# Five of 22 pairs of upward FFN tiles as seven half-width products, in a two-block transformer kernel on one core

## The reference

```python
D_FF = 2816
def conv_ffn(h, w_up, conv_w, w_down):
    gu = causal_dwconv(h @ w_up, conv_w)
    g, u = jnp.split(gu, 2, axis=-1)
    return (jax.nn.silu(g) * u) @ w_down
...
x = x + conv_ffn(rmsnorm(x, norm_ffn_gain[i]), ffn_w_up[i], ffn_conv_w[i], ffn_w_down[i])
```

## Time and profile before

| | |
|---|---|
| median of 3 runs | 1222.37 us (1222.31 to 1222.84) |
| the profiled execution | 1223.61 us, its span 1221.5 us |
| upward FFN, 22 pairs | about 795 to 1036 us of the span |
| busy share of the span | PE 99%, PEld 81%, DVE 57%, ACT 50%, POOL 57% |

### The profile page before, as it was taken

How to read it: one execution, slowest core, us unless ns; L and a number is a source line. 1 busy time by engine, 2 the same in 40 slices (tenths; PEclk the granted TensorE clock), 3 DMA queues, 4 the chain that set the end, 5 groups by cost and what they waited for, 6 DMA issues and landing times.

```text
span 1221.5 us, 18340 instructions
## 1 busy us (share of the span) xinstructions
PE 1207.6 (99%) x6667; PEld 990.1 (81%) x6667; DVE 698.6 (57%) x1239; ACT 612.0 (50%) x1184; POOL 700.3 (57%) x538
## 2 busy tenths in 40 slices
PE   9999999999999999999999999999999999999997
PEld 7977777777888899987887777878888888889886
DVE  5545426757646777745697555445454545966224
ACT  6355535676644344445634656544444444333544
POOL 8673232353269776855484566545655565886842
PEclk9999999999999999999999999999999999999999
DMA  7432222122223333354142223333333333333332
GB/s 236 107 95 73 70 61 61 52 63 77 70 62 103 95 98 94 107 179 116 52 119 58 58 62 96 96 85 104 87 88 102 103 88 80 101 96 117 108 87 69
DMA packets 62432, 112.22 MB, mean 92 GB/s; under 512 B 6856, under 2 KB 11464, under 8 KB 62344
## 3 DMA queue, kind: packets, MB, share of 16 engines
q1 hardware_dynamic: 62200, 111.06, 32.5%
q10 hardware_dynamic: 144, 0.00, 0.0%
...
## 4 chain that ended last, share of the span: by engine, by line
PE 95%; DVE 3%; ACT 1%; issue 1%; POOL 1%; DMA 0%; SPq 0%; DVEq 0%; POOLq 0%; ACTq 0%
PE pb L1101 23%; PE pb L1102 23%; PE pb L1104 23%; PE pb L1154 3%; PE pb L1156 3%; PE pb L1155 3%; PE pb L1310 2%; PE pb L1286 2%; PE pb L1163 2%; PE pb L1253 1%; PE pb L1224 1%; PE pb L1226 1%; PE pb L1225 1%; PE pb L1207 1%; PE pb L1205 1%; PE pb L1275 1%
## 5 line engine op out<-in xcount | busy, mean ns | idle before, releaser
L2684 POOL TENSOR_TENSOR wlo<-raw,whi 128x512 fp32r<-128x512 f32 (+2 forms) x384 | 518.7, 1369 | 333.2 <-ACT whi L1503 332.2
L1101 PE MATMUL pb<-HH,whi 128*128 128x512 f32 x856 | 345.4, 404 | 0.0
L1102 PE MATMUL pb<-HL,whi 128*128 128x512 f32 x856 | 338.5, 395 | 0.0
L1104 PE MATMUL pb<-HH,wlo 128*128 128x512 f32 x856 | 337.5, 394 | 0.0
L1503 ACT ACTIVATE whi<-raw 128x512 fp32r<-128x512 f32 (+2 forms) x384 | 226.1, 613 | 106.9 <-PE pb L1104 55.7
L1101 PEld LDWEIGHTS pb<-HH,whi 128*128 128x128 f32 x856 | 161.3, 188 | 42.2 <-issue 4.6
L1102 PEld LDWEIGHTS pb<-HL,whi 128*128 128x128 f32 x856 | 161.0, 188 | 38.1 <-issue 2.9
L1104 PEld LDWEIGHTS pb<-HH,wlo 128*128 128x128 f32 x856 | 160.9, 188 | 37.4
L1976 DVE TENSOR_TENSOR pb<-pb,rff 128x512 f32<-128x512 f32 x44 | 30.8, 700 | 124.0 <-PE pb L1104 117.6
L1621 ACT ACTIVATE P<-P,stat 128x256 f32<-128x256 f32 (+3 forms) x96 | 50.5, 527 | 78.7 <-DVE stat L2246 57.1
L2684 POOL TENSOR_TENSOR fl<-cv,fh 128x512 fp32r<-128x512 f32 x22 | 28.9, 1314 | 86.4 <-ACT fh L1897 86.4
...
## 6 DMA issues: line engine op xcount, KB each, us to landing
...
```

The source lines that it names most:

```text
L1101: pe.do.matmul(b, hi, xh[k], start=start, stop=False, skip_group_check=tile[0] == "down")
L1102: pe.do.matmul(b, hi, xl[k], start=False, stop=False, skip_group_check=tile[0] == "down")
L1104: m = pe.do.matmul(b, lo, xh[k], start=False, stop=stop, skip_group_check=tile[0] == "down")
L2684: g.do.tensor_tensor(lo, x, hi.bitcast(F32), ALU.subtract).then_inc(*up(name, point))
```

## The change

`UPS` names the five pairs j = 6, 9, 11, 13 and 15. Their two tiles are made by seven products.

- **Activation sums** `tus`, `tuh`, `tul` for the new pairs are made once, one quarter in each of the pairs j = 1 to 4: ScalarE scales x into SBUF and into two PSUM banks (three copies), VectorE makes four sums of 256 columns, ScalarE one high part of 1024 columns, GpSimd two low parts of 512.
- **A seven-product pair** takes three banks: `ab` (the bank of `("ffn", 0, j)`), `cd`, and `e` (the bank of `("ffn", 1, j)`). ScalarE copies the first product from `ab` to U7 only once S2 is done, and stands with that copy ahead of the split of S4. VectorE then has six instructions on the banks (`product_up`), and `scaled` follows for both tiles behind the last product.
- **Low parts**: in these pairs GpSimd makes that of S3 too, so all seven.
- **Order of steps**: `taps(1, j-1)` and `product(j-1)` move behind the product of S3 in a pair of `UPS`; `product(j-2)` moves from the first half of pair j-1 into its second half, ahead of `scaled(1, j-1)`.

```diff
+UPS = (6, 9, 11, 13, 15)
+NUP = NGATE + len(UPS)
...
         for x in FACTORS:
-            self.split_to(self.unit_of[p, x] + LOOK)
+            if not NGATE <= p < NUP or x not in ("A22", "S2"):
+                self.split_to(self.unit_of[p, x] + LOOK)
             self.add("product7", p, x)
+            if NGATE <= p < NUP and x == "S2":
+                self.split_to(self.unit_of[p, x] + LOOK)
+            if x == "S3" and NGATE <= p < NUP:
+                self.add("taps", 1, UPS[p - NGATE] - 1)
+                self.add("product", UPS[p - NGATE] - 1)
...
+                if half and j + 1 in UPS and j not in UPS:
+                    add("product", j - 1)
                 add("scaled", half, j)
-                if (half, j) != (0, 0):
-                    add("taps", 1 - half, j - 1 + half)
                 if half:
+                    add("taps", 0, j)
                     add("swish", j)
-                elif j:
-                    add("product", j - 1)
+                elif j and j not in UPS:
+                    add("taps", 1, j - 1)
+                    if j + 1 not in UPS:
+                        add("product", j - 1)
...
             def product7(p, x):
-                if p >= NGATE:
+                if kind(p) == "up" and x == "S2":
+                    a.wait_ge(*at("product7", p, x))
+                    a.wait_ge(*at("u3", p - 1))
+                    a.do.activation(U7, ps("ffn", 0, UPS[p - NGATE])[:, 0:H], ACT.Copy).then_inc(*up("a_c7", ("v0", p)))
...
+            def product_up(p, x):
...
+                if x == "S2":
+                    v.wait_ge(*at("v0", p))
+                    v.wait_ge(*at("product7", p, "S2"))
+                    plus(U7, ab[:, right], U7, ("u2", p))
+                elif x == "S3":
+                    v.wait_ge(*at("product7", p, "S3"))
+                    v.wait_ge(*last("v_c7"))
+                    plus(W8, cd[:, left], U7)
+                    plus(ZU, cd[:, right], U7, ("u3", p))
+                    v.wait_ge(*last("v_c7"))
+                    plus(e[:, right], cd[:, right], W8, ("empty", ("cd", j)))
+                    plus(e[:, left], e[:, left], ZU)
+                elif x == "S4":
+                    v.wait_ge(*at("product7", p, "S4"))
+                    plus(ab[:, right], ab[:, right], W8)
...
-                elif factor[1] == "S3":
+                elif factor[1] == "S3" and kind(factor[0]) != "up":
                     return
```

More of the change, by code:

```diff
@@ L618, in second @@
         add("begin3")
+        sums_of = {j + 1: j for j in range(4)}
         for j in range(NPAIR):
+            if j in UPS:
+                for t in (("ffn", 0, j), ("cd", j), ("ffn", 1, j)):
+                    take(t)
+                self.pair(NGATE + UPS.index(j))
             for half in range(2):
-                take(("ffn", half, j))
-                self.proj(("ffn", half, j), "ffn_up", 2816 * half + P * j)
+                if j not in UPS:
+                    take(("ffn", half, j))
+                    self.proj(("ffn", half, j), "ffn_up", 2816 * half + P * j)
                 if j == 0 and half == 0:
@@ L664, in second @@
                 self.hold(DOWN_BANK["tile"][7], ("down", 7))
-            self.pair(NGATE + n)
+            self.pair(NUP + n)
             add("down_out", 2 * n)
@@ L948, in sums_at, with kind @@
             return S7 if p < NGATE else S8
+        def kind(p):
+            return "gate" if p < NGATE else "up" if p < NUP else "down"
         T_AT = {"S1": 0, "S3": 1, "A22": 2, "S2": 3}
@@ L1004, in build @@
         ffn_work = a3.p
+        sums_places = [(ffn_work, ffn_work + 8 * T)] + [(place[f"fh{j}"], place[f"fl{j}"]) for j in (16, 18, 20)]
+        THU, TLU = ([tensor_at(f"tu{n}{kp}", [P, 2 * T], F32R, sums_places[kp][x]) [:, :] for kp in range(4)]
+                    for x, n in enumerate("hl"))
+        TSU = [tensor_at(f"tus{kp}", [P, 2 * T], F32, sums_places[kp][1])[:, :] for kp in range(4)]
+        ZU = tensor_at("zu", [P, H], F32, 226176)[:, :]
         a3.p += 4 * (4 * T + 64)
@@ L2035, in split @@
                     weights("S3", arrived["A11"], arrived["A21"], ALU.subtract)
-                elif x == "A12":
+                elif x == "A12" and kind(p) != "up":
                     w = plan.unit_of[p, "S3"]
@@ L2051, in step @@
                     v.do.tensor_tensor(dst, one, two, op).then_inc(*up("v_t7", *points))
+                if g == 3:
+                    left, right = slice(0, H), slice(H, T)
+                    one, two = (ps("ts", kp, i) for i in range(2))
+                    v.wait_ge(*at("t_scaled", kp))
+                    step(x11, one[:, right], x11, ALU.subtract, ("empty", ("ts", kp, 0)))
+                    step(x12, two[:, right], x12, ALU.subtract)
+                    v.wait_ge(*last("v_t7"))
+                    step(x22, two[:, right], x11, ALU.subtract)
+                    v.wait_ge(*last("v_t7"))
+                    step(x21, two[:, left], x22, ALU.subtract, ("t_raw", g, kp), ("empty", ("ts", kp, 1)))
+                    return
+                xhs, xls = ((hh, hl), (FH, FL))[g]
                 if g:
@@ L2091, in product7 @@
             def product7(p, x):
-                if p >= NGATE:
-                    return product8(p, x)
+                if kind(p) != "gate":
+                    return product8(p, x) if kind(p) == "down" else product_up(p, x)
                 one, two = PAIRS[p]
@@ L2593, in scaled @@
                 b = ps("ffn", half, j)
-                v.wait_ge(*at("full", ("ffn", half, j)))
+                if j in UPS:
+                    v.wait_ge(*last("v_c7"))
+                else:
+                    v.wait_ge(*at("full", ("ffn", half, j)))
                 v.wait_ge(*at("rff"))
```

72 lines of the change are left out of this document (58 added, 14 removed).

## The result

| | us, median (lowest to highest) | runs |
|---|---|---|
| before | 1222.41 (1222.25 to 1224.17) | 11 |
| changed | 1225.52 (1225.21 to 1227.37) | 11 |

The ratio is 1.0025, with a 95% interval of 1.0015 to 1.0034: **slower by 3.1 us**, 0.25%. The forecast was 1222.9 us and "same"; the time lies inside the whole range given, 2.6 us above the forecast, but 0.7 us outside the 1219.9 to 1224.8 us of the likeliest case, and beyond the 2.4 us that the prediction took for no change.

A forecast was written before the change was run, and what follows sets the result against it. TensorE, busy 99% of the span, was taken as the bound: 1223.61 - 6.27 gained + 6.8 new waits = 1224.1 us for the profiled execution, given as a 1222.9 us median; range 1216.0 to 1227.5 us.

The forecast's parts named there:

- The gain: TensorE, five upward pairs: 9.90 us for 11.154 each, 6.27 us saved if operands are there in time.
- A pair without lateness: Seven-product pair, VectorE on time: S4's low part ends about 8.1 us after the first matmul, wanted at 8.28; fits by 0.2.
- all seven instructions: VectorE's two swishes, two products, S1, S2, S3, all operands in SBUF: nearly every one stretched by GpSimd's subtractions.
- c: Mean stretch of one of seven VectorE instructions with all operands in SBUF that meet GpSimd's subtractions; 0.58 us taken.
- b = 7c - 0.3: VectorE's lateness at a seven-product pair's first matmul T, `scaled` being due at T+0.27; 0.3 us is the room to spare.
- The lower bound: Least mean stretch, 0.29 us, from how far the gate stage's four sums' medians exceed 0.684 us.
- beyond b = 0.8 or so: Seven-product pair: past this VectorE lateness in us, TensorE waits one for one, at A12 or at S4.
- the second rival: VectorE and GpSimd step in phase, so the second of each couple and S4's sum pay 0.90 us; 1227.4 us; chance 0.24.
- Pair 6 has no such pair ahead of it [...]: nothing: TensorE at pair 6: no new wait, since no seven-product pair precedes it; pair 9, behind two plain pairs, none either.
- if pairs 6 or 9 wait as well: Stated sign of being wrong: TensorE waits in these two pairs, forecast at 9.9 us each.
- the activation sums cost nothing: Pairs 1 to 4: added work of 2.7 us ScalarE, 1.7 VectorE, 2.6 GpSimd is covered, costing TensorE nothing.
- The copy: ScalarE's U7 copy, 0.37 us, starts a five-step chain of 3.39 us; S4's split and next units' splits queue behind it.

The follow-up runs named there:

- e7: Changed kernel with tanh's result and the swish in a PSUM bank instead of SBUF; 1223.53 us, 1.0004 of the kernel before.
- e1: Changed kernel with seven products in pairs 7, 10, 13 and 16 instead of 6, 9, 11, 13 and 15; 1220.23 us, 0.9979 of the kernel before.
- e5: Changed kernel with the activations' four quarter sums made in pairs 0 to 3 instead of 1 to 4; 1225.32 us, 1.0024 of the kernel before.
- e3: Changed kernel with ScalarE's copy of S2's product and VectorE's addition behind the last factor's split again; 1222.71 us, 1.0002 of the kernel before.

## Why the prediction was right or wrong

**The gain** was a little larger: 9.74 us a pair, not the 9.90 of the gate, 5 x (11.154 - 9.744) = 7.05 for 6.27 us. (The starts in the earlier trace rows are those of the second tiles of their pairs, which begin at 801.41 and 1024.54; the 11.154 us stay.)

**A pair without lateness** fits, as worked out: in pair 9 S4's low part ended at 898.31, and the sum gave T + 8.28 = 898.63 as the time when it is wanted, 0.3 us to spare for 0.2.

**The stretch and the lateness** came out at the size forecast, in part by luck. That all seven instructions are exposed, not only the sums of the earlier trace rows, is shown by 1045 for 692 ns and by e7, which takes the stretch from two of them by moving an operand; the Trainium skill (SBUF — State Buffer, Who interferes with whom) has it so, and these rows agree. The mean stretch of the seven was 0.56 us ahead of pair 11 and 0.60 ahead of 13 and 15, for c = 0.58; b = 7c - 0.3 = 3.76 us was forecast for pair 11 and 3.76 measured; for 13 and 15, 1.1 us less, 2.7, and measured 2.74 and 2.77. But c stood for seven that all meet GpSimd. In fact the last swish and product ahead of these pairs were not stretched (0.68 and 0.69 us), since GpSimd then waited 1.35 to 1.64 us for S3's split, and the other five made up for it with 0.15 to 1.16 us each. The lower bound was misread: c = 0.29 takes the medians of the earlier trace rows for a mean, while the gate stage's 28 sums took 1.21 us in the mean, which is c = 0.52. And 7.23 + 4 x 0.42 + 1.5 is 10.41, not 10.35: 0.2 us to spare, not 0.3.

**From lateness to wait.** The step "beyond b = 0.8 or so" was too generous. Lateness of `scaled` against T + 0.27, and the pair's length over 9.744:

| run, pair | b, us | wait, us |
|---|---|---|
| changed, 6 / 9 / 11 | 2.49 / -0.07 / 3.76 | 2.34 / 0 / 3.30 |
| changed, 13 / 15 | 2.74 / 2.77 | 2.24 / 2.31 |
| e1, 7 / 10 / 13 / 16 | 1.96 / -0.07 / 0.97 / 1.16 | 1.51 / 0.05 / 0.54 / 0.67 |
| e5, 6 | 2.31 | 1.86 |
| e7, 11 / 15 | 2.65 / 2.56 | 2.19 / 2.10 |

TensorE waits one for one from about 0.45 us on (in pair 6 from 0.15). The working had S4's sum at 0.68 us; released by a copy that comes with A12's low part, it took 1.57 us in pair 6 and 1.25 to 1.26 in 11, 13 and 15. So far the second rival came true, and also in the second of each couple where GpSimd was at work: ahead of pairs 11, 13 and 15 the first product and S2 were 0.91 to 1.12 us over 0.69. The three waits were 3.30 + 2.24 + 2.31 = 7.85 for 6.8 us.

**The step that failed** is "Pair 6 has no such pair ahead of it [...]: nothing", and by the prediction's own signs ("if pairs 6 or 9 wait as well") it is wrong there: pair 6 waited 2.34 us. The lateness was counted from a seven-product pair behind, but S1, S2, S3, swish and product, five of the seven that are stretched, stand in the plain pair right ahead of any such pair, and need only a GpSimd subtraction under way as they start. That pair 9 was right was luck of phase: GpSimd was idle as the swish began. e1 shows the same in pairs 7, 13 and 16. With this, "the activation sums cost nothing" fell by 0.47 us (e5), not by the whole of pair 6.

**The sum** with the measured terms: 7.85 + 2.34 - 7.05 = +3.1 us, which is the difference of the medians; in the traces the stretch from the first upward matmul to the first downward one grew as much, from 1035.68 - 788.56 = 247.12 to 1037.61 - 787.32 = 250.29 us. Against the forecast, pair 6 gave +2.3, the smaller room +1.05, the larger gain -0.8.

**The copy.** The prediction named what is queued behind it, but priced only the chain. e3 gives it a price: with VectorE 2.5 to 3.4 us late ahead of the four pairs that wait, the copy ahead of S4's split cost 2.8 us against the copy behind.
